# Retention stage of a hybrid decoder step: key tiles over three PSUM banks, an own buffer for masked sample keys, and another order of units, sample work and VectorE work

## What is computed

```python
def step(S, qkv):                       # one chunk of 128 tokens
    qc, kc, vc = qkv
    att = jnp.einsum('bihd,bjhd->bhij', qc, kc) * dmat[None]
    o = (jnp.einsum('bhij,bjhe->bihe', att, vc)
         + jnp.einsum('bihd,bhde->bihe', qc, S) * q_decay[None, :, :, None])
    S = (chunk_decay[None, :, None, None] * S
         + jnp.einsum('bjhd,bjhe->bhde', kc * k_decay[None, :, :, None], vc))
    return S, o
...
mu = jnp.mean(o_r, axis=-1, keepdims=True)
var = jnp.mean(jnp.square(o_r - mu), axis=-1, keepdims=True)
o_r = ((o_r - mu) * lax.rsqrt(var + EPS)).reshape(B, T, R_V) * gn_g.astype(jnp.float32)
```

## Time and profile before

| | us |
|---|---|
| three runs | 1009.57, 1013.23 (median), 1014.15 |
| profiled execution, its time | 1012.44 |
| its span in the trace | 1010.7 |
| PE busy | 942.0 (93% of the span) |
| DVE busy | 556.4 (55%) |
| ACT busy | 338.7 (34%) |
| POOL busy | 203.6 (20%) |
| mean DMA rate | 217 GB/s |

### The profile page before, as it was taken

The page is one execution under the profiler, slowest core; times in us unless marked ns, Lnnn a source line. Parts: engine busy times, 40 slices in busy tenths (PEclk is TensorE's granted clock), DMA queues, the critical chain, the costliest instruction groups (busy, mean ns, idle before and its releaser), DMA issues.

```text
span 1010.7 us, 19785 instructions
## 1 busy us (share of the span) xinstructions
PE 942.0 (93%) x7032; PEld 870.6 (86%) x7032; DVE 556.4 (55%) x1015; ACT 338.7 (34%) x518; POOL 203.6 (20%) x171
## 2 busy tenths in 40 slices
PE   4999999999999999999999999989789999998992
PEld 4998999899989998977786787777659999998991
DVE  3348624953484449466755766776765333433248
ACT  4124403431342144324433533443455334333100
POOL 0037103601450154041041141032010000000003
PEclk9999999999999999999989999999969999999897
DMA  8995499459846965535844862863766887786972
GB/s 258 219 304 178 153 206 317 145 166 199 285 145 196 209 245 172 176 112 188 307 138 163 293 208 93 297 219 117 250 230 215 276 279 249 237 300 220 374 267 93
DMA packets 162514, 219.73 MB, mean 217 GB/s; under 512 B 8336, under 2 KB 136080, under 8 KB 160656
## 3 DMA queue, kind: packets, MB, share of 16 engines
q1 hardware_dynamic: 157776, 205.90, 66.4%
q0 software_dynamic: 4048, 11.02, 3.4%
q10 hardware_dynamic: 656, 2.36, 0.6%
HBM read 206.53 MB, written 100.01 MB: 303 GB/s over the span
## 4 chain that ended last, share of the span: by engine, by line
PE 74%; DVE 12%; issue 7%; POOL 4%; DMA 2%; ACT 1%; DVEq 0%; SPq 0%; POOLq 0%; ACTq 0%
PE bank L734 18%; PE bank L736 17%; PE bank L735 17%; PE bank L1011 4%; PE bank L729 4%; PE bank L764 3%; PE bank L846 2%; DVE wl L1411 2%; DVE part_l L1637 2%; PE bank L1056 2%; PE bank L1047 1%; DVE scoresp L1486 1%; DVE fsum L1542 1%; DMA xn<-in_x_prompt_dram 1%; PE bank L1080 1%
## 5 line engine op out<-in xcount | busy, mean ns | idle before, releaser
L734 PE MATMUL bank<-xh,wh 128*128 128x288 f32 x640 | 192.6, 301 | 3.3 <-DVE vn L1475 2.9
L734 PE MATMUL bank<-wh,xh 128*128 128x256 f32 x640 | 187.5, 293 | 3.5 <-DVE wl L1411 3.0
L736 PE MATMUL bank<-xh,wl 128*128 128x288 f32 x640 | 189.6, 296 | 0.0
L735 PE MATMUL bank<-xl,wh 128*128 128x288 f32 x640 | 189.5, 296 | 0.0
L736 PE MATMUL bank<-wh,xl 128*128 128x256 f32 x640 | 183.1, 286 | 0.0
L735 PE MATMUL bank<-wl,xh 128*128 128x256 f32 x640 | 182.9, 286 | 0.0
L1411 DVE TENSOR_TENSOR wl<-raw,wh 128x1024 fp32r<-128x1024 f32 (+1 forms) x104 | 128.2, 1268 | 48.1 <-ACT wh L1185 38.1
L734 PEld LDWEIGHTS bank<-wh,xh 128*128 128x128 f32 x640 | 124.7, 195 | 6.4 <-issue 3.6
L1185 ACT ACTIVATE wh<-raw 128x1024 fp32r<-128x1024 f32 (+1 forms) x104 | 101.6, 1018 | 82.6 <-PE bank L764 40.4
L734 PEld LDWEIGHTS bank<-xh,wh 128*128 128x128 f32 x640 | 121.3, 190 | 7.0 <-DVE vn L1475 6.3
L735 PEld LDWEIGHTS bank<-wl,xh 128*128 128x128 f32 x640 | 124.6, 195 | 1.2
(11 more groups left out here) (212 smaller groups left out, 1776.4 us busy)
## 6 DMA issues: line engine op xcount, KB each, us to landing
raw<-in_w_in_dram SPq DMA_DIRECT2D x128, 256.0 KB
cslot<-in_cache_kv_w_dram SPq DMA_DIRECT2D x32, 1024.0 KB, 6.2
out_dram<-in_cache_kv_w_dram SPq DMA_DIRECT2D x32, 1020.0 KB, 9.7
out_dram<-in_cache_kv_w_dram SPq DMA_DIRECT2D x12, 2040.0 KB, 10.4
far<-in_cache_kv_w_dram SPq DMA_DIRECT2D x32, 512.0 KB, 10.3
raw<-in_w_in_dram SPq DMA_DIRECT2D x16, 512.0 KB
out_dram<-in_cache_kv_w_dram SPq DMA_DIRECT2D x3, 2720.0 KB, 18.8
out_dram<-in_cache_kv_w_dram SPq DMA_DIRECT2D x16, 504.0 KB, 4.8
```

What stands on the lines that cost most here:

```text
L734: pe.matmul(out, lhs[0](k), rhs[0](k), start=(k == 0), stop=False)
L735: pe.matmul(out, lhs[0](k), rhs[1](k), start=False, stop=False)
L736: last = pe.matmul(out, lhs[1](k), rhs[0](k), start=False, stop=(k == n - 1))
```

## The change

It has six parts, all in stage B; no instruction with work in it is added or taken away.

1. Key tiles 0 to 4 go to banks 2, 3, 0, 2, 3 (`KEY_BANK`) instead of 2, 3, 2, 3, 2. A tile waits for the tile three before it, tile 2 for the last unit in bank 0.
2. `km` is a buffer of its own, and POOL's wait for `rt_done` 4 goes.
3. In `cached_output(1)` the next units stand ahead of tiles 3, 6 and 9 instead of 4, 8 and 11, and the prompt's `ro` transposes ahead of tile 12 instead of behind tile 13.
4. `value_unit(0)` moves from the head's start into the seam of the head before, between the next head's first key tiles and the sample `ro` transposes; for the first head it stands ahead of the loop.
5. `cached_turn(1)` follows the sample `ro` transposes instead of preceding them.
6. DVE takes the statistics of prompt and sample rows together, ahead of tile 0; the split of the next value weights (`low`, line 1411) comes after tile 5 instead of 8, `normalise` after tile 8 instead of 10; at the end `retained(0)`, `retained(1)`, `output_sum`, `values(0)` of the next head, `retained(2)`, `retained(3)`, `output` instead of `output_sum`, `retained(0)`, `output`, `retained(1..3)`.

```diff
+KEY_BANK = (2, 3, 0, 2, 3)
...
+        km = sb("km", [NS, DEC_B * RK], F32, scope_b)
...
-        km = rot[0:NS].rearrange("p a b -> p (a b)")[:, 0:DEC_B * RK]
...
                 pool.wait_ge(kd_done, r + 2)
-                pool.wait_ge(rt_done, r * 18 + 4)
...
-                if j >= 2:
-                    pe.wait_ge(part_low, r * (2 * PARTS) + (PARTS * x + PARTS + j - 1))
+                if j == 2:
+                    pe.wait_ge(unit_free, r * B_UNITS + (3 + U_B + 5 + 4 * x))
+                if j > 2:
+                    pe.wait_ge(part_low, r * (2 * PARTS) + (PARTS * x + PARTS + j - 2))
                 for h in range(H):
-                    last = turn(bank[2 + j % 2][:, h * P:(h + 1) * P], cslot[s][:, k, h * DH:(h + 1) * DH])
+                    last = turn(bank[KEY_BANK[j]][:, h * P:(h + 1) * P], cslot[s][:, k, h * DH:(h + 1) * DH])
...
-                chunk_ready(r * B_CH + (C0_B + 1))
-                value_unit(0)
                 cached_scores(0)
...
-                cached_output(1, [(4, lambda: next_unit(2)), (8, lambda: next_unit(3)), (11, lambda: next_unit(4))])
-                pe.wait_ge(normed, r + 1)
-                for e in range(2):
-                    b = group(14 + e)
-                    blocks(lambda t, c: turn(b[:, c], ro[:, t, e * P:(e + 1) * P]))
+                def normed_prompt():
+                    pe.wait_ge(normed, r + 1)
+                    for e in range(2):
+                        b = group(14 + e)
+                        blocks(lambda t, c: turn(b[:, c], ro[:, t, e * P:(e + 1) * P]))
+
+                cached_output(1, [(3, lambda: next_unit(2)), (6, lambda: next_unit(3)), (9, lambda: next_unit(4)),
+                                  (12, normed_prompt)])
                 if not last_head:
                     transpose_tile(r + 1, 0, 0)
                     transpose_tile(r + 1, 0, 1)
-                cached_turn(1)
+                    sample_values(B_UNITS, r)
                 for e in range(2):
                     b = group(16 + e)
                     settle(pe)
                     turn(b[:, 0:NS], ro[0:NS, QBLK, e * P:(e + 1) * P]).then_inc(rt_done, 1)
-
+                cached_turn(1)
+
+            def sample_values(n, r):
+
+                chunk_ready(r * B_CH + (n // B_UNITS * B_CH + C0_B + 1))
+                natural(1, r * B_UNITS + (n + U_B + 5 + 2), QBLK, 1)
+
+            sample_values(0, 0)
             transpose_tile(0, 0, 0)
             transpose_tile(0, 0, 1)
...
-                prompt_statistics()
+                statistics()
                 next_projected(0)
                 probs(1)
                 lows(1, 1, 0, 3)
                 next_projected(1)
-                sample_statistics()
-                lows(1, 1, 3, 7)
-                next_projected(2)
-                lows(1, 1, 7, 9)
+                lows(1, 1, 3, 6)
                 if not last:
                     low(r * B_CH + (C0_B + 3), 1)
-                lows(1, 1, 9, 11)
+                next_projected(2)
+                lows(1, 1, 6, 9)
                 normalise()
                 next_projected(3)
-                lows(1, 1, 11, VTILES)
+                lows(1, 1, 9, 12)
                 next_projected(4)
+                lows(1, 1, 12, VTILES)
+                retained(0)
+                retained(1)
                 output_sum(1)
-                retained(0)
+                if not last:
+                    values(0, B_UNITS)
+                for n in (2, 3):
+                    retained(n)
                 output(1)
-                for n in (1, 2, 3):
-                    retained(n)
```

33 lines of the change are left out of this document (17 added, 16 removed).

## The result

The changed kernel took **994.76 us** (median of 4 runs, 993.70 to 996.00) against 1011.43 (4 runs, 1009.57 to 1014.15): ratio **0.9844, 95% interval 0.982 to 0.9868**. A second series of the same kernel gave 1000.67 (4 runs, 997.00 to 1002.81), ratio 0.9874 (0.9836 to 0.9912), which is inside the range; all eight have their middle at 996.5. The profiled execution of the first series took 993.70 us, its span is 992.0 against 1010.7.

A forecast was written before the change was run, and what follows sets the result against it. PE was taken as the bound (busy 93%), its stage B pauses as the direct win. Terms 3.6 + 4.8 + 2.3 - 0.8 + 2.3 = 12.2 us off 1012.44, plus 0.8 for the median, gave 1001.0; range 996 to 1009.5.

The forecast's parts named there:

- The mask: Sample output in stage B: POOL masks early enough that PE's four waits for it go; win 3.6 us, lower bound 2.4.
- Value tiles of x = 1: Three heads, first value tile to next key transposes: 17.1 us becomes 15.5 without waits; win 4.8 us in all.
- The seam: Three times, key transposes to next unit: 11.4 us against 13.4, 11.7 and 11.4, despite a new 1.1 us wait; win 2.3.
- The third bank: Key tiles: x = 1 gains 0, its fifth tile waiting for DVE's state chain; any x = 0 gain is counted elsewhere.
- The rule on banks: Key tiles: rotating independent groups through PSUM banks overlaps evacuation; by it 5.0 us of waits would go, the prediction expected little.
- Entry: Ahead of stage B's loop: the sample unit no longer covers the first key tiles' way through ACT and DVE; loss 0.8 us.
- Last head: End of stage B: `ro` transposes move into the pause ahead of tile 12, large `retained` run beside PE; win 2.3 us.
- Only reordered: Last head: DVE's work up to tile 13 is the same in another order, so tile 13's part is ready at 744.2 as before.
- The clock: Stage B: the 3.4 us pieces at half clock, eight counted at 1.7 us each under full PE work, keep their old number.
- VectorE late in the value tiles: PE waits for a full DVE in value tiles and seams; win only 4.0 us, time 1009.2; chance 0.19.
- Banks the limit: Key tiles wait for banks, not DVE: 4.1 us more win in heads and seams, time 996.9; chance 0.08.
- Slower by the clock: Two half-clock pieces behind each of 8 score stretches, 16 in all: 15.3 us more, time 1016.3; chance 0.04.

The follow-up runs named there:

- the better seam: Changed kernel with `cached_turn(1)` directly behind the two key tiles, the sample unit last, and `output` and two low parts ahead of `values(0)` on VectorE: 997.54 us, 0.9858.
- the fillers: Kernel before plus matmuls whose results nobody reads in TensorE's pauses of stage B, every wait and other instruction kept: 1007.03 us, ratio 0.9940.
- seam with bank: Kernel before with parts 1, 4, 5 and the seam's share of part 6 alone: 1007.70 us, ratio 0.9958.
- the value tiles alone: Kernel before with part 3 and part 6 up to tile 13 alone, the seam as before: 1011.84 us, ratio 1.0010.

## Why the prediction missed, point by point

- *The mask.* Predicted 3.6 us, 0.9 a head. Clean S1 fell by 1.0 in each head (41.9 to 40.95). Right.
- *Value tiles of x = 1.* Predicted 15.5 us from the first tile to the key transposes, a win of 1.6. Measured 15.25 in all three heads (642.77 to 658.02 in the third), a win of 1.8, 5.5 in all, with no wait in them. Right, and the walk through VectorE's queue held.
- *The seam.* Predicted 11.4 us each and a new wait of 1.1, ended by `output`. Measured 12.1, 11.0, 10.9 and waits of 1.34, 1.33, 1.19. The gain was 2.5 us against 2.3 predicted. The mechanism is right. That the sum agrees so well is in part luck: the clean seams are 0.4 shorter than predicted, and the first had a half-clock piece of 1.2 us that the prediction didn't have there. The step that put `output` behind `values(0)` is the one that the better seam then undid.
- *The third bank.* Predicted 0 for x = 1. The fifth key tile there waits 0.81 as before. Right. But in x = 0 the bank is worth 0.6 us a head with the new seam, since without it the transposes wait for a part that comes after `output`. The rule on banks (the Trainium skill, Perfetto Trace Analysis, Matmuls) fits the key tiles of x = 0 in the seam, and not those of x = 1.
- *Entry.* Predicted a loss of 0.8; from the start of stage B to the first own-key products it was 19.1 and is 19.7, a loss of 0.6. Right in sign and about in size.
- *Last head.* Predicted 2.3. From its output groups to the end of B 25.8 us before and 24.05 after, 1.75. Somewhat less. "Only reordered" was not harmless here: the statistics of the sample rows (0.41) and the aggregation (0.44), which VectorE now does ahead of tile 0, stand in front of the probabilities and low parts that TensorE is waiting for, so the first value tile waits 3.55 instead of 2.63 and the stretch ahead of it took 0.9 longer. The tail took 2.7 less.
- *The clock: the step that failed.* "The half-clock pieces behind the score stretches I leave at their old number." 34.6 us of stage B were at half clock, and 13.7 are; that is ten pieces' worth before, not the eight that the prediction counted, and four now. In the first three heads seven became two, which is 5 us of time, the size of the fillers' gain on the kernel before (5.4 in B). The sum of the terms was 12.2; with 5.0 added it is 17.2, and B lost 17.3; that two single executions match so closely is partly luck. The prediction had named the argument (denser value tiles speak for fewer, the thin seam for more) and took nought as the middle between them, though most of its terms took pauses away and only the seam and the entry put any in. Its price for a piece, 1.7 us, also holds only where TensorE works without a pause: measured are 1.5 in S1 and S3 and 0.1 in S2. In the second series, where 23.9 us stayed at half clock, B took 321.0, and the prediction's own terms gave 322 (334.2 - 12.2). So in the series in which more pieces came back the forecast is right to 0.3 us (1000.67 against 1001.0), and the range was left by what stayed away in the first. That agreement is luck as well: stage A took 4.3 us more in that profiled execution, and 23.9 us at half clock are still not the old number.
- *What stood in no term:* with the clock up, the output groups can't go faster than 11.0 us (S2), since TensorE then waits for the weights of unit 0. The two new waits of 1.3 for `wl` are that. The half-clock piece that lay there before cost nearly nothing, 0.1 us, and two of them 1.4.
- *Rivals.* VectorE late in the value tiles: not seen in the first three heads. Banks the limit: 996.9 was near the time, but the waits at the fifth tile (x = 1) are unchanged, so it was near for another reason. Slower by the clock: the clock mattered, with the other sign; stage B has four pieces where that rival had sixteen.
- *Adding up.* The terms were priced one by one, and as clean stretches they nearly add: value tiles 1.3, seam with bank 0.65, together 2.3 us of S3 (27.0 to 24.7). As times they don't: the value tiles alone gave 1.001, and taken away from after they cost 6.9 us of B. In these runs a gain in waits was paid out only where the stretch behind it held the clock and wasn't waiting for VectorE itself.

## What to carry to other kernels

Price a pause of TensorE at its length plus a share of the half-clock pieces that such pauses bring (here 12 us for the pauses, 5 for the clock in one series and 2 to 3 in the other), and where most terms remove pauses, don't leave the pieces at their old number. To split the two before rearranging anything, fill the pauses with matmuls that nobody reads: what the time falls by is the clock's share. Measure single parts by stretches without a half-clock piece, not by the total or by one execution, and when a wait moves, look at what stands in front of the wanted instruction in its engine's queue.

## What the runs showed that was not expected

- 23 extra matmuls a head in the pauses made the kernel before faster, by 5.4 us in stage B.
- A half-clock piece costs 1.5 us where TensorE is the bound (S1, S3), and 0.1 where it would wait for VectorE anyway (S2).
- The parts taken one by one barely move the mean clock; together they do.
- The first head of stage A has two lengths. In 15 of 18 profiled executions its attention products begin at 101.1 to 103.7 us, in three at 106.9 to 107.3, whatever the kernel; all heads behind take 97.4 us each. In after, of the waits of TensorE between 60 and 110 us:

```profile
PE bank L734 <- DVE vn L1485: 0.7, 1, 0.7
```

In its second series, one of the three:

```profile
PE bank L734 <- DVE vn L1485: 2.3, 1, 2.3
PE bank L729 <- DVE qt L1458: 0.9, 1, 0.9
PE bank L764 <- DVE kv L1473: 0.6, 1, 0.6
```

A half-clock piece at 104.0 in the second one adds 1.5. What makes VectorE late there was not tried. It made 4.3 of the 9.1 us between the two profiled executions of after; where the pieces of stage B fell made 4.2. Whether the same two make the 6 us between the medians of the two series, only profiles of all runs could tell.
